# Where the mixing scale is applied: from the rows before the product to the readers after it

## What is computed

```python
def rmsnorm(x, w):
    y = xf * lax.rsqrt(jnp.mean(xf * xf, axis=-1, keepdims=True) + EPS)
    return (y * w).astype(x.dtype)

hn = rmsnorm(h, norm_mix_w)                    # h: 256 x 1024, the output of the second layer norm
q, k, v, z, xbc, dt_raw = split(hn @ w_in)     # 1024 x 4112
att = chunk_band_attention(q, k, v, rel_bias)
ssd = ssd_mixer(z, xbc, dt_raw, ...)           # conv, silu, scan, gate by silu(z), group norm
h = h + concatenate([att, ssd]) @ w_out
h = h + square(relu(rmsnorm(h, norm_mlp_w) @ w_ff1)) @ w_ff2
```

## Time and profile before

| | us |
|---|---|
| median of 3 runs | 781.71 (780.65 to 781.85) |
| the profiled execution | 780.67 |
| its span, first to last instruction | 778.9 |
| TensorE busy | 762.0 (98%) |
| VectorE busy | 513.8 (66%) |
| ScalarE busy | 416.0 (53%) |
| GpSimd busy | 98.3 (13%) |
| mean granted TensorE clock | 0.998 |

### The profile page before, as it was taken

One profiled execution on the slowest core, in us unless ns is written; L12 is line 12 of the kernel. 1 busy time (PEld: TensorE's weight loads), 2 busy tenths in 40 slices (PEclk: granted clock), 3 DMA queues, 4 the chain that ended last, 5 costly groups with the idle time before them and its releaser, 6 DMA issues.

```text
span 778.9 us, 12960 instructions
## 1 busy us (share of the span) xinstructions
PE 762.0 (98%) x5014; PEld 670.3 (86%) x5014; DVE 513.8 (66%) x816; ACT 416.0 (53%) x623; POOL 98.3 (13%) x74
## 2 busy tenths in 40 slices
PE   8999999999999999999999899999999999999997
PEld 7998877799978887999787699889777999999996
DVE  6985556666664558477866875787856755555554
ACT  5544445453664553446675567576655544444443
POOL 3341000000100004111300207700000000000002
PEclk9999999999999999999999999999999999999999
DMA  9965643344664544676833554765317575656541
GB/s 334 332 203 177 215 163 108 122 157 121 210 224 160 172 157 160 195 227 197 247 114 104 166 176 151 219 205 173 109 55 219 192 237 191 207 177 211 169 156 55
DMA packets 77659, 139.54 MB, mean 179 GB/s; under 512 B 7184, under 2 KB 15648, under 8 KB 77600
## 3 DMA queue, kind: packets, MB, share of 16 engines
q1 hardware_dynamic: 75744, 132.15, 52.4%
q0 software_dynamic: 1856, 6.57, 2.6%
HBM read 134.90 MB, written 1.06 MB: 175 GB/s over the span
## 4 chain that ended last, share of the span: by engine, by line
PE 87%; DVE 6%; issue 3%; POOL 2%; ACT 1%; DMA 1%; SPq 0%; POOLq 0%; ACTq 0%; DVEq 0%
PE acc L1081 13%; PE acc L1083 13%; PE acc L1082 13%; PE acc L1089 12%; PE acc L1091 12%; PE acc L1090 12%; DVE w_lo L810 2%; PE acc L1369 1%; PE acc L1403 1%; DMA raw<-in_w_in_even 1%; PE acc L1342 1%; PE acc L1282 1%; PE acc L1238 1%; PE acc L1353 1%; POOL b_lo L810 1%
## 5 line engine op out<-in xcount | busy, mean ns | idle before, releaser
L810 DVE TENSOR_TENSOR w_lo<-raw,w_hi 128x1024 fp32r<-128x1024 f32 (+1 forms) x224 | 275.3, 1245 | 171.3 <-ACT w_hi L790 90.2
L1089 PE MATMUL acc<-x_hi,w_hi 128*128 128x256 f32 x840 | 234.8, 280 | 1.5 <-DVE w_lo L810 1.1
L1091 PE MATMUL acc<-x_hi,w_lo 128*128 128x256 f32 x840 | 232.1, 276 | 0.0
L1090 PE MATMUL acc<-x_lo,w_hi 128*128 128x256 f32 x840 | 232.1, 276 | 0.0
L790 ACT ACTIVATE w_hi<-raw 128x1024 fp32r<-128x1024 f32 (+1 forms) x128 | 133.6, 1045 | 126.4 <-PE acc L1091 63.9
L780 ACT ACTIVATE w_hi<-raw 128x1024 fp32r<-128x1024 f32 x109 | 116.1, 1065 | 107.6 <-PE acc L1091 55.5
L1089 PEld LDWEIGHTS acc<-x_hi,w_hi 128*128 128x128 f32 x840 | 157.7, 188 | 4.1 <-issue 2.8
L1090 PEld LDWEIGHTS acc<-x_lo,w_hi 128*128 128x128 f32 x840 | 157.8, 188 | 0.8 <-issue 0.5
L1091 PEld LDWEIGHTS acc<-x_hi,w_lo 128*128 128x128 f32 x840 | 157.7, 188 | 0.0
L1081 PE MATMUL acc<-w_hi,cat_hi 128*128 128x512 f32 x272 | 108.9, 400 | 0.2 <-DVE w_lo L810 0.2
L1083 PE MATMUL acc<-w_hi,cat_lo 128*128 128x512 f32 x272 | 106.2, 390 | 0.0
(11 more groups left out here) (297 smaller groups left out, 903.0 us busy)
## 6 DMA issues: line engine op xcount, KB each, us to landing
raw<-in_w_ff SPq DMA_DIRECT2D x32, 1024.0 KB, 5.3
raw<-in_w_in_even SPq DMA_DIRECT2D x28, 1024.0 KB, 5.0
raw<-in_w_in_odd SPq DMA_DIRECT2D x16, 1024.0 KB, 5.4
raw<-in_w_in SPq DMA_DIRECT2D x16, 1024.0 KB, 5.6
raw<-in_w_out_even SPq DMA_DIRECT2D x12, 1024.0 KB, 5.4
raw<-in_w_out SPq DMA_DIRECT2D x4, 1024.0 KB, 5.3
raw<-in_w_in_even SPq DMA_DIRECT2D x4, 512.0 KB, 6.2
raw<-in_w_ukv_even SPq DMA_DIRECT2D x8, 256.0 KB, 3.2
```

The costliest lines, as they stand in the source:

```text
L810: ins = eng.tensor_tensor(lo, r, hi.bitcast(F32), ALU.subtract)
L1089: pe.matmul(o, wh[k][:, fs], hi[:, ka, :], start=start and f % 2 == 0, stop=False, skip_group_check=True)
L1090: pe.matmul(o, wh[k][:, fs], lo[:, ka, :], start=False, stop=False, skip_group_check=True)
L1091: ins = pe.matmul(o, wl[k][:, fs], hi[:, ka, :], start=False, stop=stop, skip_group_check=True)
```

## The change

It has five parts, and all of them are in the second block.

1. The mixing scale. `row_scaled` is gone. TensorE turns `res` itself, and `x_hi`, `x_lo` are the unscaled rows with the gain. Each reader of a product that depends on them multiplies by r. A result with tokens in the partitions takes a column of r (v, z, dt, and the gate, where z's factor is used); one with features in the partitions takes `r_row`, a 128 x 256 tile with r of each token along its columns: a product of a matrix of ones with diag(r) (`mix_spread`), copied to SBUF by ScalarE. The readers of conv, q and k move from ScalarE to VectorE for this.
2. The passage. The turns of t = 0 and t = 1 use different banks of `aux`. The products of v are in another order: first those of t = 0 with `x_hi`, then the low ones of t = 0 among the high ones of t = 1, last the low ones of t = 1. dt is one pass over 256 tokens, where it was two over 128. `keep_busy` is called once, with four.
3. The far product goes to banks 0 and 1 of `aux`, and its input is made ahead of the second set of `ssd_xs`.
4. The gate: VectorE defers the split of weights around `ssd_last`, `ssd_gate`, `ssd_scale` and `ssd_turn`, ScalarE around `ssd_turn`; the gated rows are scaled and turned in two halves.
5. Weights of a piece with 256 columns are shifted in the weight buffer, as those of feature chunks were.

```diff
-BUSY_MIX = (5, 1)
+BUSY_MIX = 4
...
+            step("mix_spread", 0)
             step("dt_sum", c_dt)
             step("epi", c_dt)
...
-    between = [[("ssd_cb", 0), ("ssd_xs", 0), ("ssd_xs", 1)], [("ssd_rows", 0)], ...
+    between = [[("ssd_cb", 0), ("ssd_xs", 0), ("ssd_far", 0), ("ssd_xs", 1)], [("ssd_rows", 0)], ...
         two()
+        if ("ssd_gate", 0) in sts:
+            step("ssd_scale", 0)
...
-            p.shift = (80, 112) if p.chunk.layout == "feat" else (0, 0)
+            p.shift = (80, 112) if p.chunk.layout == "feat" or p.cols == S else (0, 0)
...
+            def v_rows(p, t):
+                if t == 0:
+                    for b in range(4):
+                        high(0, b)
+                    return
+                for b in range(4):
+                    low(0, b)
+                    high(1, b)
+                for b in range(4):
+                    ins = low(1, b)
...
-                    pe.wait_ge(*due("mix_scaled", 2 * t + h + 1))
+                    pe.wait_ge(*due("mix_row", 2 * t + h + 1))
                     for k in range(4 * h, 4 * h + 4):
-                        ins = pe.transpose(aux[:, k // 2, ...], rows[:, k * P:(k + 1) * P], ident)
+                        ins = pe.transpose(aux[:, 2 * t + h, ...], res[:, t, k * P:(k + 1) * P], ident)
...
+                elif kind == "mix_spread":
+                    pe.wait_ge(*due("mix_diag", 1))
+                    own(pe.matmul(aux[:, 3, 0:S], ones, gated[:, 1, :], start=True, stop=True), "mix_spread")
...
-                            ins = pe.matmul(aux[:, 2 + g, :], cb[:, 2, g, :],
+                            ins = pe.matmul(aux[:, g, :], cb[:, 2, g, :],
...
+                    elif c.epilogue == "conv_in":
+                        dve.wait_ge(*due("piece_used", c.pieces[-1].n + 1))
+                        dve.wait_ge(*due("row_scale", 1))
+                        for b in range(2):
+                            ins = dve.tensor_tensor(conv_in[:, f:f + 2, 3:], a2[:, b, :]..., rows_scale(2), ALU.mult)
...
-                    row_mean_square(0)
                     row_part(0, 1)
...
-                    row_lo(0, 0, 2)
                     row_normed(1)
-                    row_lo(0, 2, 4)
+                    row_lo(0)
+                    row_mean_square(0)
                     row_mean_square(1)
+                    row_lo(1)
                     low_prep(dt_piece.n)
-                    row_lo(1, 0, 4)
                     low_prep(conv_piece.n)
+                    dve.wait_ge(*due("mix_r", T))
```

More of the change, by code:

```diff
@@ L141, in __init__ @@
         self.banks = None
+        self.scaled = False
 def plan(w):
@@ L547, in build @@
     by_turn = {c.turn: c for c in chunks if c.turn is not None}
-    READER = {"keep_ranks": "act", "copy_tok": "act", "copy_feat": "act", "conv_in": "act", "copy_dt": "dve"}
+    after_mix = min(c.n for c in chunks if c.epilogue == "copy_dt") - 1
+    for c in chunks:
+        c.scaled = c.acts == "x" and c.n >= after_mix and c.epilogue != "relu2"
+    READER = {"keep_ranks": "act", "copy_tok": "act", "copy_feat": "act", "conv_in": "dve", "copy_dt": "dve"}
     reads = {"act": 0, "dve": 0}
@@ L553, in build @@
             c = s[1]
-            c.reader = "act" if c.info.get("table") == 1 else READER.get(c.epilogue, "dve")
+            c.reader = "act" if c.info.get("table") == 1 else "dve" if c.scaled and c.layout == "feat" else READER.get(c.epilogue, "dve")
             reads[c.reader] += 1
@@ L842, in build @@
         mix_at = [s[0] for s in steps].index("mix_rows")
-        v_piece, dt_piece, *_ = [s[1][0] for s in steps[mix_at:] if s[0] == "rows_of"]
+        v_piece, *_, dt_piece = [s[1][0] for s in steps[mix_at:] if s[0] == "rows_of"]
         conv_piece = pieces[dt_piece.n + 1]
-        waiting = {at for at, (s0, s1) in enumerate(zip(steps, steps[1:])) if s0[0] in ("piece", "rest") and s1[0] in ("scores", "ssd_cb")}
+        waiting = {at for at, (s0, s1) in enumerate(zip(steps, steps[1:])) if s0[0] in ("piece", "rest") and s1[0] in ("scores", "ssd_cb", "ssd_last", "ssd_turn")}
+        scale_at = [s[0] for s in steps].index("ssd_scale")
+        waiting.add(max(at for at in range(scale_at) if steps[at][0] == "rest"))
         held = {s0[1].n for s0, s1 in zip(steps, steps[1:]) if s0[0] == "piece" and s1[0] == "mlp_split"}
@@ L1141, in rows_of @@
                 hi, lo = acts[c.acts]
-                if p is c.pieces[0] and t == 0:
+                if p is c.pieces[0] and (t == 0 or p is dt_piece):
                     before = by_turn[c.turn - 2]
@@ L1556, in _ @@
                         hi_first(act, own, conv_piece.n + 1)
+                elif kind == "mix_spread":
+                    act.wait_ge(*due("mix_spread", 1))
+                    own(act.activation(r_row, aux[:, 3, 0:S], ACT.Copy), "row_scale")
                 elif kind == "mix_end":
@@ L1584, in _ @@
                     a2 = acc[:, c.pair, :, 0:c.width] if c.layout == "tok" else acc[:, c.pair, :, :]
-                    if c.epilogue in ("copy_tok", "copy_feat"):
+                    if c.scaled and c.epilogue == "copy_tok":
                         act.wait_ge(*due("piece_used", c.pieces[-1].n + 1))
-                        scale = DH ** -0.5 if c.acts == "x" and c.info["dst"] == ("R3", 0) else 1.0
-                        own(act.activation(epi_dst(c), a2, ACT.Copy, scale=scale), "acc_read_act")
+                        act.wait_ge(*due("mix_r", T))
+                        for t in range(T):
+                            ins = act.activation(epi_dst(c)[:, t], a2[:, t], ACT.Copy, scale=mix_r[:, t:t + 1])
+                        own(ins, "acc_read_act")
+                    elif c.scaled and c.epilogue == "silu_tok":
+                        act.wait_ge(*due("piece_used", c.pieces[-1].n + 1))
+                        act.wait_ge(*due("mix_half", 1))
+                        for t in range(T):
+                            ins = act.activation(epi_dst(c)[:, t], a2[:, t], ACT.Tanh, scale=half_r[:, t:t + 1])
+                        own(ins, "tanh_ready")
+                    elif c.epilogue in ("copy_tok", "copy_feat") and not c.scaled:
+                        act.wait_ge(*due("piece_used", c.pieces[-1].n + 1))
+                        own(act.activation(epi_dst(c), a2, ACT.Copy), "acc_read_act")
                     elif c.epilogue.startswith("silu"):
@@ L1611, in _ @@
                     elif c.epilogue == "conv_in":
-                        act.wait_ge(*due("piece_used", c.pieces[-1].n + 1))
                         act.wait_ge(*due("pad_ready", 1))
-                        for b in range(2):
-                            f = c.info["dst"] + 2 * b
-                            ins = act.activation(conv_in[:, f:f + 2, 3:], a2[:, b, :].rearrange("p (f s) -> p f s", f=2), ACT.Copy)
-                        own(ins, "acc_read_act")
-                        own.wait()
+                        act.wait_ge(*due("acc_read_dve", c.read_count))
                         m = c.info["dst"] // 4
```

157 lines of the change are left out of this document (97 added, 60 removed).

## The result

The changed kernel takes **777.55 us** (median of 6, 776.63 to 778.15), the kernel before 781.23 beside it (780.58 to 781.85): 0.9948 of the time, 95% interval 0.9935 to 0.9961, or 3.7 us less. The forecast was 778.8 and 2.9 us less, with a range of its own of 777.9 to 779.8. The profiled execution has a span of 774.8 us, where it was 778.9.

What follows compares the result with a forecast made beforehand. TensorE, busy 762.0 of 778.9 us, was taken as the bound, so gains were its waits and useless products. Terms 2.5 - 0.5 - 0.3 + 0.8 + 0.4 = 2.9 us took 781.71 to 778.8; own range 777.9 to 779.8, wider 777.2 to 780.6.

Steps and rivals of the forecast that it cites:

- the rival on dt: dt bound by issue, not streaming: groups stay 0.24 us apart, dt takes 1.0; 778.0, or 777.7 with the shift; chance 0.13.
- VectorE is now the chain: Passage: VectorE's x_lo and dt's split, ending at 446.2, pace the remaining v products and so the start of dt.
- the far product's 0.8: Scan: moving the far product's input ahead of two VectorE instructions removes TensorE's wait; gain 0.8 us (0.7 to 0.9).
- the time of GpSimd's root in the gate: Gate: from VectorE's start at 539.7 to the scaling takes 4.1 us as before, so the root is there at 543.8.
- The passage: From the block's last product to the first conv piece, which starts at 448.25, not 450.77; gain 2.5 us (1.8 to 3.4).
- dt: Passage: with 256 columns the group step doubles to 0.45 us, so dt takes 1.9 us against 2.0 before.
- mix_spread and the convolution: mix_spread behind the first conv piece loses 0.5 us (0.4 to 0.7); VectorE's later copies lose 0.3 (0 to 1.0).
- The gate: Near product to first band scores: one split, not two, behind the scaling, so cat_lo begins earlier; gain 0.4 us (0 to 0.9).
- The shift: Second half of v: shifted weights could save 0.3 us, but inside the gate's chain set by VectorE; nothing, 0.3 at most.
- The clock: Rival in the passage: granted clock falls from 2.4 to 1.2 GHz at 439 to 443; 784.2 us, chance 0.05.

Runs made afterwards that it cites:

- lo_gap: The changed kernel with the first two of sixteen x_lo instructions moved into VectorE's idle gap ahead of the t = 1 rows; 777.58 us.
- sq_fix: The changed kernel with ScalarE's squares of t = 1 behind x_hi and VectorE's mean of them behind the sixth x_lo; 777.60 us.
- conv_act: The changed kernel with the convolution's input copied by ScalarE again, as a plain copy without the rows' scale; 777.70 us.
- no_far: The changed kernel with the far product put back behind the second turns' copies, in banks 2 and 3; 778.86 us.
- busy0: The changed kernel without the eight useless products (keep_busy) ahead of the second turns of the gated rows; 778.10 us.
- root_gap: The changed kernel with two x_lo instructions of t = 0 moved between the variance and the centring of t = 1; 778.09 us.
- sq_late: The changed kernel with ScalarE's squares of t = 1 behind x_hi and VectorE's mean of them behind dt's split; 778.89 us.
- g2: The changed kernel with VectorE's deferred split moved behind the scaling of the gated rows, so GpSimd's root runs beside k's read; 777.70 us.
- again: The changed kernel itself measured once more, unedited; 777.60 us, median of five.
- g3: g2 with one of the two deferred splits moved behind cat_lo, the other still behind the scaling; 776.91 us.

## Where the prediction failed, and where it held

The kernel takes 777.55, 1.25 us below the forecast and below its own range of 777.9 to 779.8. Of this, 0.48 is no matter of the change: the forecast started from 781.71, and the kernel before took 781.23 beside the new one. The other 0.77 is gain that the sum lacks: 3.68 us measured (the interval amounts to 3.0 to 5.1), 2.9 forecast. The wider range of 777.2 to 780.6 does hold the result, but it reached so low for the sake of the rival on dt, which the trace refutes, so that is luck.

In the stretches the sum is 0.60 too small: 0.27 in the passage, 0.24 at the far product, 0.17 in the gate and 0.06 in the convolution, less 0.14 at the second turns. The direction of each of the five was right. The step of the mechanism that failed is "VectorE is now the chain", in the passage, and the largest term beside it that was mis-sized is the far product's 0.8. A second step was wrong without a cost, the time of GpSimd's root in the gate.

- **The passage, 2.5 forecast, 2.77 measured.** The first turns start at once, the second at 6.04 us from the start (6.0 forecast), `x_hi` of t = 1 ends at 9.46 (9.7). The step that failed is "VectorE is now the chain". It had `x_lo` end 11.5 us from the start, with v's last product behind it at 11.8 and dt at 11.95; they came at 10.92, 11.53 and 11.74. VectorE needs no such time: the two small instructions and the sixteen `x_lo` took 4.36 us from the first start to the last end, where the forecast had 4.85, and lo_gap changed their order and nothing moved. The chain is rows, ScalarE's squares and `x_hi`, and then TensorE itself: thirty products at 0.12 to 0.13 us from 441.79 to 445.57. sq_fix shows the part of ScalarE: 0.35. Dt took 1.87 where 1.9 stood.
- **dt.** Four groups 0.43 to 0.46 apart, forecast 0.45: for 256 columns the step about doubles, as streaming says. The rival, that a group costs its issue and would still take 0.24, is out, and with it the 0.8 us that the Trainium skill's rule of some 60 cycles for each matmul (TensorEngine Tiling (Array Packing), Performance Considerations) would have given as the prediction applied it; the measured step decides.
- **mix_spread and the convolution.** 0.44 and 0.44, forecast 0.5 and 0.3; conv_act shows that they are two separate things. Of the second, VectorE reached `L2363` 0.44 later against TensorE (forecast 0.29): the tanh of z is what it waits for (1.65 at `L2021`). With the copies back on ScalarE `L2021` begins 0.02 ahead of the first product of C and B, with them on VectorE 0.84 behind.
- **The far product.** The wait went, as forecast. It was sized by its row, 0.8, with 0.7 to 0.9 as its range, and was worth 1.04: 0.93 from start to start and 0.11 in the far product itself (no_far, above). The passage and this are the greater part of what the sum lacks.
- **The gate.** 0.57, forecast 0.4. The scaling begins 7.17 us behind the fourth near product (541.40 less 534.23), forecast 545.0 less 537.72, 7.28, and `cat_lo` 9.88 behind it, forecast 10.03. That the number is nearly right is partly luck. The prediction had the root ready at 543.8, on the ground that it took as long as before, which is 6.08 behind the fourth near product; it came at 7.02 (541.25 less 534.23), since the split that fills VectorE's wait stretches it from 1.04 to 1.99. K's read ends just then and hides it. The prediction didn't ask what a VectorE instruction moved beside GpSimd does to GpSimd, though the earlier trace rows held the hint: 1.51 us for one column.
- **The shift.** Nothing, as forecast: 24 of v's products ahead of the turn take 2.71 us where they took 2.76, and TensorE then waits 0.56 for the turn.
- **The clock.** Granted 1.00 through the passage, and in busy0 too.
- **The rest of the difference.** Ahead of the passage, the thirteen profiles of kernels with the same work there reach it between 433.59 and 435.32 us. In the pair of the result 0.56 of the 4.1 us between the profiles is of this kind; read as an effect it would have made the change look better than it is.

## What to carry to other kernels

Ask of each instruction that fills a wait what runs beside it, and not only what stands behind it: here a small operation of GpSimd became 1 to 2 us longer beside VectorE instructions that read two operands in SBUF. Size a wait of TensorE from start to start, not by its row: here 1.04 us for a row of 0.8. When a stall goes, name the next chain by two finish times that can be compared (here `x_lo` at 10.9 us and v's last product at 11.5), and test it by filling the gap. Where an unrelated part of the program varies by more than the effect, measure between two products of the bottleneck engine: stretches repeated within 0.05 us here, whole runs within 1.9.

## What the hardware showed that was not expected

- **GpSimd's root beside VectorE.** One column (128x1) took 0.54 us with VectorE on `x_lo`, whose operands are one in PSUM and one in SBUF (sq_fix, root_gap); 1.52 beside the centring, 1024 columns with two operands in SBUF; 2.59 beside two such splits (sq_late). Four columns took 1.05 beside a read from PSUM (g2) and 1.99 beside one split. That read is as long as the split, 1.22 us for 1024 columns, so it is the operands and not the length that tell. It ended 0.41, 0.40 and 0.91 us behind the end of the VectorE work in the three bad cases, so that it seems to do nothing until that is over. The Trainium skill names this contention (GPSIMD Engine Reference, Specifications: the SBUF interfaces are shared with VectorE, in conflict with instructions with two SBUF inputs), and the traces agree with it in all of these cases; that VectorE itself was not slowed (1.22 for one split and 2.35 for two, as elsewhere) they show too.
- **The clock.** 2.43 us in which TensorE did nothing, between v's products and the turns (busy0), cost no granted clock: 1.00 in every window of the passage.
- **The start of the program.** The six runs of the result fall into two groups about 1.1 us apart (776.63 to 777.08 and 778.02 to 778.15; before, 780.58 to 780.74 and 781.71 to 781.85); the five of `again` spread as far, less cleanly (776.43, 776.71, 777.60, 777.65, 778.36). In the profiles the like arises in the first 20 us, when the first pieces land: in the thirteen profiles of the changed kernel and its variants one and the same product (2600 ahead of the passage) starts between 18.77 and 20.76, and the passage between 433.59 and 435.32. The first product of those pieces starts at 7.47 and 7.40 us in the two profiles of the changed kernel, and at 8.46 with a wait of 0.43 for its split in g3. Why was not tried.
